# Hybrid decoder step on one core: prompt attention heads in pairs on two row halves and two column groups, with the forget bias copied to all partitions by DMA

## The chip, the core and the metric

The kernel runs on one core of one Trainium2 chip. Its time is the device time of one launch in microseconds, the median of several runs.

## What is computed

One inference step of one hybrid layer for a prompt (1 x 256 tokens) and eight samples (8 tokens each, with 256 cached tokens), all float32, width 1024, 16 heads of 64. The part that matters here is the forgetting attention of the prompt:

```
ft = cumsum(logf)                        # per head, over the 256 tokens
for blk in (0, 1):                       # 128 queries each
    sc   = q[blk] @ k[:kend].T * scale   # kend = 128, then 256
    bias = ft[blk, :, None] - ft[None, :kend]
    p    = softmax(where(mask, sc + bias, -inf))
    out  = p @ v[:kend]
```

The query's own term `ft[q]` is the same for a whole row of the softmax, so both kernels add only `-ft[k]` (`Fp`). Around it stand: adaLN gains from a conditioning vector, one input projection (recurrent input, q, k, v, forget logits, two gates), a convolution and RG-LRU scan, the samples' attention over cached pages, an output projection, and a mixture of 32 experts (top 4) in blocks.

## The kernel before, in words

Five engine programs are written out by hand in `hybrid_layer`, one per engine, with semaphores between them. Nothing schedules them: the order is the text's.

`JOBS` is TensorE's list of projections. It ends with v, four rows of gains, q (eight jobs of 16 passes: a float32 matmul is two passes), then `GATES`: eight jobs for `gbT` and eight for `gaT`, one beside each prompt head (`gate_job`, L1355, matmul L1361). Weights come in chunks of 128 x 8 x 512 floats (2 MB), three buffers in turn. SP issues chunk c when chunk c - 3 has been used (`chunk`, L335). Chunks 18 and 19 hold q, 20 to 23 the gates, 24 and 25 the output projection.

The heads of the prompt, TensorE L1373 to L1410: `scores(h)` writes bank h % 3 with four matmuls, q and k of the head (64 rows, the upper or lower half of the array by h % 2; L1379) and, for the bias, a one-hot column of `ident` against `Fp` (16 rows, L1380), for 128 and for 256 keys. VectorE's `head_max` (L880) adds `mask` and takes two maxima, ScalarE's `exps` (L580) exponentiates, `head_norm` (L890) divides, TensorE's `weights` (L1383) turns three squares of 128, ScalarE copies them out (L592), and `values` (L1391) multiplies them with v in `tok`: 64 columns, the pair's two heads in the two halves of bank 7 one iteration apart. `head_out` (L897) gates a pair and frees the bank. Three heads are in flight in `Ssb`.

```
for h in range(H):          # TensorE, L1404
    gate_job(h)
    if h + 2 < H:
        scores(h + 2)
    if h >= 1:
        values(h - 1)
    weights(h)
```

After it come the cached forget logits (L1419, L1421), their cumulative sum `Fs` on VectorE (L922 to L930), and the samples: keys turned by `keysT`, scores by `sscores` (L1449). `work` first holds the convolution's input and the scan's `A` and `U`, later the samples' `KT`; `rg_free` tells that the scan is over. `F_made` tells that `Fp` (1) and `Fs` (2) are made.

SP's order around the stage: chunks 7 to 21, sixteen small copies of cached forget rows (L357), chunks 22 to 25, then the pages of keys and values.

Of the kernel before, what the change touches and what calls it, by code (L numbers as in the profile page):

```python
# [31 lines left out]
def hybrid_layer(nc, x_prompt, x_sample, cache_k, cache_v, cache_logf, state_conv, state_h, page_table,  # L32
# [35 lines left out]
    with ctx:  # L68
# [32 lines left out]
        Ssb = fr[:, 0:1152].rearrange("p (s n) -> p s n", s=3)  # L101
# [24 lines left out]
        U = Uf.rearrange("p (t c) -> p t c", t=NT)  # L126
        vrows = work[:, 5900:6540].rearrange("p (g n) -> p g n", g=5)
# [81 lines left out]
        Fs = hf[:, 0:2 * (PAST + DS)].rearrange("p (s c) -> p s c", s=2)  # L209
# [8 lines left out]
        nm = few(66, 6).rearrange("p (s n) -> p s n", s=3)  # L218
        rsum = few(72, 6).rearrange("p (s n) -> p s n", s=3)
# [22 lines left out]
        def vec(name, n=NT):  # L242
# [7 lines left out]
            scores_ps scores_read negmax_made exp_done probs_made PT_ps PT_ev py_ps py_read  # L250
# [64 lines left out]
        def _(eng):  # L315
# [23 lines left out]

            for c in range(7):  # L340
                chunk(c)
# [11 lines left out]
            for c in range(7, 22):  # L353
                chunk(c)
# [4 lines left out]
            for c in range(22, len(CHUNKS)):  # L359
                chunk(c)  # L360
            eng.wait_ge(s["rg_free"], 1)

# [15 lines left out]

            keys_in(0)
            keys_in(1)  # L380
            for b in range(DB):
                values_in(b)
                if b + 2 < DB:
                    keys_in(b + 2)
# [29 lines left out]
        def _(eng):  # L414
# [46 lines left out]
            eng.wait_ge(s["rg_free"], 1)  # L461
            for i in range(2):
                eng.tensor_copy(KT[:, i, :, PAST:PAST + NS], kT[:, :, SP_:T]).then_inc(s["tailk_made"], 1)
# [51 lines left out]
        def _(eng):  # L515
# [50 lines left out]
            for j in range(GATES):  # L566
                job(j)
                if j == LAST["f"]:
                    eng.wait_ge(s["absw_made"], 2)
                    A_(Ssb[0:H, 0, 0:T], Ssb[0:H, 0, 0:T], ACT.Exp, scale=-1.0).then_inc(s["expw_made"], 1)  # L570
# [9 lines left out]
            def exps(h):  # L580
                eng.wait_ge(s["negmax_made"], h + 1)
                P = Ssb[:, h % 3, :]
                link(A_(P[:, 0:128], P[:, 0:128], ACT.Exp, bias=nm[:, h % 3, 0:1], accum_out=rsum[:, h % 3, 0:1]))
                A_(P[:, 128:384], P[:, 128:384], ACT.Exp, bias=nm[:, h % 3, 1:2],
                   accum_out=rsum[:, h % 3, 1:2]).then_inc(s["exp_done"], 1)

            exps(0)
            exps(1)
# [115 lines left out]
        def _(eng):  # L704
# [123 lines left out]
            w_, t_, x_ = Ssb[0:H, 1, 0:T], Ssb[0:H, 0, 0:T], Ssb[0:H, 2, 0:T]  # L828
# [13 lines left out]
            for g in range(4):  # L842
                q = 32 * g
                V_.tensor_copy(hsel[q:q + H, :].rearrange("k (h c) -> k h c", c=DS),
                               ident[q:q + H, q:q + H].unsqueeze(2).to_broadcast([H, H, DS])).then_inc(s["hsel_made"], 1)

# [22 lines left out]
            eng.wait_ge(s["consts_made"], 5)  # L869
            link(V_.tensor_tensor_scan(Fp, onesf[0:H, 0:SP_], lfz[:, 0:SP_], 0.0, ALU.mult, ALU.add))  # L870
            TS(Fp, Fp, -1.0, None, ALU.mult).then_inc(s["F_made"], 1)
            ada_rows(8)
            ada_rows(9)
# [3 lines left out]
            ada_rows(10)  # L877
            ada_rows(11)

            def head_max(h):  # L880
                eng.wait_ge(s["scores_ps"], h + 1)
                if h >= 3:
                    eng.wait_ge(s["PT_ps"], h - 2)
                P = Ssb[:, h % 3, :]
                TTo(P, B[h % 3][:, 0:384], mask, ALU.add).then_inc(s["scores_read"], 1)
                eng.wait_ge(s["scores_read"], h + 1)
                link(V_.tensor_reduce(nm[:, h % 3, 0:1], P[:, 0:128], AX.X, ALU.max, negate=True))
                V_.tensor_reduce(nm[:, h % 3, 1:2], P[:, 128:384], AX.X, ALU.max, negate=True).then_inc(s["negmax_made"], 1)

            def head_norm(h):  # L890
                eng.wait_ge(s["exp_done"], h + 1)
                P, r_ = Ssb[:, h % 3, :], rsum[:, h % 3, :]
# [15 lines left out]
            head_max(0)  # L908
            head_max(1)
            for h in range(H):  # L910
                head_norm(h)
                if h + 2 < H:
                    head_max(h + 2)
                if h % 2 and h >= 3:
                    head_out(h // 2 - 1)
                if h > NT:
                    gated(h - NT - 1)
            gated(NT - 1)
            eng.sem_inc(s["rg_done"], 1)

            eng.wait_ge(s["tr_ps"], G_CF + 1)
            link.later(V_.tensor_copy(Fs[:, :, 0:PAST], B[2][:, :].rearrange("p (s c) -> p s c", s=2)))  # L922
# [7 lines left out]
            TS(Fs, Fs, -1.0, None, ALU.mult).then_inc(s["F_made"], 1)  # L930
            head_out(H // 2 - 1)
# [290 lines left out]
        def _(eng):  # L1222
# [128 lines left out]
            eng.wait_ge(s["st_made"], 1)  # L1351
            for g in range(G_ST, G_CF):
                transposes(g)

            def gate_job(h):  # L1355
                j = GATES + h
                eng.wait_ge(s["job_ev"], j - 1)
# [10 lines left out]
            eng.wait_ge(s["F_made"], 1)  # L1368
            eng.wait_ge(s["tr_ev"], G_CF)
            eng.wait_ge(s["adaF_made"], 8)  # L1370
            eng.wait_ge(s["job_ev"], GATES)

            def scores(h):  # L1373
                p, o = h // 2, 64 * (h % 2)
                if h >= 3:
                    eng.wait_ge(s["scores_read"], h - 2)
# [27 lines left out]
            for h in range(H):  # L1404
# [3 lines left out]
                if h >= 1:  # L1408
                    values(h - 1)
# [359 lines left out]
```

## Time and profile before

| | us |
|---|---|
| median of 3 runs | 1550.29 (1547.12 to 1553.09) |
| the profiled execution | 1547.08 |
| its span | 1545.4 |
| TensorE busy, matmuls | 1430.2 |
| VectorE, ScalarE, GpSimd busy | 341.8, 231.4, 25.3 |

The span is the time from the first to the last instruction of the profiled execution. A busy TensorE is no TensorE at its peak: the granted clock (PEclk) can be half, and passes of few columns can wait for their weights. The stages are, by the chain of waits: projections and scan to 263, the heads of the prompt 264 to 416, the samples and the router to 583, the experts to 1530.

### The profile page before, as it was taken

What the parts mean: (1) busy time and instruction counts of PE and PEld (TensorE: products, weight loads), DVE (VectorE), ACT (ScalarE), POOL (GpSimd) and SP (SyncE); (2) the same over time, 40 slices, a digit from 0 to 9 for tenths busy, and PEclk for the clock granted to TensorE, in tenths of its full rate; (3) what the DMA queues carried; (4) which work ended last, traced back from release to release, by engine and by line L of the source; (5) the groups of instructions that cost most, each with busy time, mean ns of one, the idle gap of its engine ahead of it and who ended that gap; (6) DMA issues with size and microseconds to landing.
All of it is one profiled execution on the core that took longest, in us unless ns stands there. A gap on an engine that the chain in (4) does not pass through costs nothing.

```text
span 1545.4 us, 15974 instructions
## 1 busy us (share of the span) xinstructions
PE 1430.2 (93%) x6379; PEld 655.4 (42%) x6379; DVE 341.8 (22%) x693; ACT 231.4 (15%) x461; POOL 25.3 (2%) x55
## 2 busy tenths in 40 slices
PE   6899899999898899999999999999999999999996
PEld 2555356555544643443443433433433433433332
DVE  3441411222323421210210210210120111121114
ACT  2112301211134321110111110111110101100102
POOL 1100001000000010000000000000000000000000
PEclk9899799888998879999999999999999999999999
DMA  8736354111323576999999999999999999999992
GB/s 297 229 142 244 117 218 150 55 55 59 112 82 110 178 322 261 420 429 427 426 428 428 426 427 421 427 428 427 426 428 426 425 428 413 424 430 428 427 426 91
DMA packets 68252, 483.67 MB, mean 313 GB/s; under 512 B 10237, under 2 KB 10981, under 8 KB 43604
## 3 DMA queue, kind: packets, MB, share of 16 engines
q1 hardware_dynamic: 66500, 477.69, 75.4%
q0 software_dynamic: 1680, 4.91, 1.0%
q8 instruction: 58, 0.95, 0.2%
q14 instruction: 14, 0.11, 0.0%
HBM read 478.48 MB, written 4.10 MB: 312 GB/s over the span
## 4 chain that ended last, share of the span: by engine, by line
PE 75%; DMA 17%; DVE 3%; issue 2%; ACT 2%; SPq 1%; DVEq 0%; ACTq 0%; PEldq 0%
PE bank L1683 33%; DMA ring<-in_w_gate_up_dram 17%; PE bank L1334 9%; PE bank L1361 5%; PE bank L1648 4%; PE bank L1226 4%; PE bank L1649 3%; PE bank L1671 2%; PE bank L1517 2%; PE bank L1317 2%; PE bank L1379 1%; PE bank L1380 1%; PE bank L1474 1%; PE bank L1397 1%; PE bank L1449 1%
## 5 line engine op out<-in xcount | busy, mean ns | idle before, releaser
L1683 PE MATMUL bank<-ring,work 128*64 128x512 f32 x2048 | 454.1, 596 | 19.6 <-issue 10.1
L1683 PEld LDWEIGHTS bank<-ring,work 128*64 128x64 f32 x2048 | 160.8, 137 | 291.2 <-issue 291.1
L1683 PE MATMUL bank<-ring,hT 128*64 128x512 f32 x1024 | 235.4, 606 | 16.4 <-DMA ring<-in_w_gate_up_dram 16.4
L1203 DVE TENSOR_TENSOR gbT<-gbT,bank 128x512 f32<-128x512 f32 x85 | 58.4, 687 | 449.0 <-PE bank L1671 388.4
L1334 PE MATMUL bank<-hT,ring 128*128 128x320 f32 x512 | 143.5, 440 | 5.7 <-DVEq L780 4.9
L1683 PEld LDWEIGHTS bank<-ring,hT 128*64 128x64 f32 x1024 | 77.4, 139 | 162.6 <-issue 162.6
L1334 PEld LDWEIGHTS bank<-hT,ring 128*128 128x128 f32 x512 | 97.8, 193 | 53.3 <-issue 6.8
L1172 DVE TENSOR_SCALAR work<-bank 128x512 f32<-128x512 f32 x32 | 22.0, 686 | 328.4 <-PE bank L1683 328.4
L1361 PE MATMUL bank<-hT,ring 128*128 128x320 f32 x256 | 82.2, 480 | 0.0
L1648 PE MATMUL bank<-qT,tok 128*128 128x256 f32 x256 | 72.4, 405 | 0.0
L1671 PE MATMUL bank<-work 128*128 128x512 f32 x136 | 67.4, 618 | 1.2 <-ACT work L694 1.2
L682 ACT ACTIVATE work<-bank 128x320 f32<-128x320 f32 x16 | 7.0, 437 | 407.7 <-PE bank L1226 407.7
L1361 PEld LDWEIGHTS bank<-hT,ring 128*128 128x128 f32 x256 | 54.0, 217 | 22.8 <-issue 7.9
L1648 PEld LDWEIGHTS bank<-qT,tok 128*128 128x128 f32 x256 | 43.4, 189 | 32.2 <-issue 28.9
L694 ACT ACTIVATE work<-bank 128x512 f32<-128x512 f32 x32 | 17.4, 594 | 217.6 <-PE bank L1683 217.6
L1226 PE MATMUL bank<-ident,ring 128*128 128x128 f32 (+2 forms) x187 | 35.6, 338 | 11.5 <-ACT work L601 7.4
L1226 PE MATMUL bank<-ident,work 128*128 128x128 f32 (+3 forms) x205 | 36.0, 299 | 10.6 <-DMA work<-in_state_conv_dram 10.6
L685 ACT ACTIVATE work<-work 128x512 f32<-128x512 f32 x32 | 20.2, 630 | 170.6 <-DVE work L1172 170.6
L1649 PE MATMUL bank<-qT,tok 64*128 64x256 f32 x128 | 44.5, 428 | 0.0
L1317 PE MATMUL bank<-ring 128*32 128x512 f32 x192 | 29.6, 709 | 13.5 <-ACT gbT L544 7.0
L1671 PEld LDWEIGHTS bank<-work 128*128 128x128 f32 x136 | 22.9, 189 | 45.1 <-issue 41.7
L1226 PEld LDWEIGHTS bank<-ident,work 128*128 128x128 f32 (+3 forms) x205 | 25.1, 184 | 32.9 <-issue 32.6
(334 smaller groups left out, 954.4 us busy)
## 6 DMA issues: line engine op xcount, KB each, us to landing
ring<-in_w_gate_up_dram SPq DMA_DIRECT2D x128, 2048.0 KB, 15.0
ring<-in_w_down_dram SPq DMA_DIRECT2D x64, 2048.0 KB, 17.1
ring<-in_w_ada_dram SPq DMA_DIRECT2D x12, 2048.0 KB, 8.0
ring<-in_w_in_dram SPq DMA_DIRECT2D x12, 2048.0 KB, 9.9
ring<-in_cache_k_dram SPq DMA_DIRECT2D x16, 512.0 KB, 5.6
ring<-in_cache_v_dram SPq DMA_DIRECT2D x16, 512.0 KB, 4.5
ring<-in_w_out_dram SPq DMA_DIRECT2D x2, 2048.0 KB, 7.7
out_dram<-tok POOLq DMA_DIRECT2D x2, 1024.0 KB, 5.2
```

What stands on the lines that cost most here:

```text
L685: A_(sig[:, 512 * j:512 * j + 512], glu[:, 512 * j:512 * j + 512], ACT.Sigmoid, scale=ALPHA)\
L1172: TS(glu[:, half[j]], B[j][:, :], LIMIT, None, ALU.min).then_inc(s["glu_made"], 1)
L1203: TTo(piece(gbf, n), piece(gbf, n), B[6 + n % 2][:, :], ALU.add).then_inc(s["scatter_read"], 1)
L1226: return nc.tensor.transpose(out, in_, ident[0:rows, 0:rows])
L1317: last = mm(ps[32 * g:32 * g + 32, :], silu_c[:, k, :], w[0][:, k, :], start=(k < 4), stop=(k >= 4))
L1334: last = mm(ps[:, 0:T], w[0][:, k, 128 * (t % 4):128 * (t % 4) + 128], hT[:, k, :], start=(k == 0), stop=(k == NT - 1))
L1361: last = mm(B[4 + h % 2][:, 0:T], w[0][:, k, 128 * (h % 4):128 * (h % 4) + 128], hT[:, k, :], start=(k == 0), stop=(k == NT - 1))
L1517: last = mm(B[5 + t][:, :], gaT[:, k, 128 * t:128 * t + 128], w[h][:, k, :], start=(k == 0), stop=(k == NT - 1))
L1648: mm(out, tok[:, k, 128 * m:128 * m + 128], sel[:, k, :], start=(k == 0), stop=False)
L1649: last = mm(out, tok[q:q + 64, 2, 128 * (m % 4):128 * (m % 4) + 128], sel[q:q + 64, 2, :], start=False, stop=True)
L1671: last = mm(bank[:, :], C[:, 128 * k:128 * k + 128], Ysb[:, 512 * (n % 2):512 * (n % 2) + 512], start=True, stop=True)
L1683: last = mm(bank[CAP * x:CAP * x + CAP, :], lhsT[:, CAP * x:CAP * x + CAP], rhs(x), start=start, stop=stop)
```

## The change

- TensorE handles heads in pairs. `scores(p)` issues both heads' matmuls of one size one after the other, on the row halves 0 to 63 and 64 to 127, into banks 2 (p % 2) and 2 (p % 2) + 1, without the bias matmuls. `values(p)` issues both heads' on the two column halves of bank 7. `weights` uses bank 6 alone.
- The bias comes by DMA. SP copies row h of `Fp` to all 128 partitions of `biasF[:, h % 8]`, 128 columns and 256 columns, two transfers a head; VectorE's `masked` adds the causal mask to them, eight heads first, then four and four. `head_max` adds `biasF` in place of `mask`.
- Four heads are in flight. `Ssb` and `biasF` now lie in `work`, behind `rg_free`; `Fs` takes the old place in `ring`.
- `Fp` is made right after the forget logits. The state transposes and the gains' rows 8 to 11 move ahead of the last four q jobs. The cached forget logits and their sum move ahead of the last gate job. POOL's copies of the samples' own keys wait for the heads that use `work`.
- SP's issues are put in another order (below).

```diff
+        biasF = work[:, 0:3072].rearrange("p (s n) -> p s n", s=8)
+        Ssb = work[:, 3072:4608].rearrange("p (s n) -> p s n", s=4)
...
+            def bias_rows(a, z):
+                for h in range(a, z):
+                    row = Fp[h:h + 1, :]
+                    eng.dma_start(biasF[:, h % 8, 0:128], row[:, 0:128].unsqueeze(1).to_broadcast([1, 128, 128])).then_inc(s["bias_in"], 16)
+                    eng.dma_start(biasF[:, h % 8, 128:384], row.unsqueeze(1).to_broadcast([1, 128, 256])).then_inc(s["bias_in"], 16)
...
-            for c in range(7, 22):
+            for c in range(7, 20):
+                chunk(c)
+            eng.wait_ge(s["F_made"], 1)
+            eng.wait_ge(s["rg_free"], 1)
+            bias_rows(0, 8)
+            for c in range(20, 22):
                 chunk(c)
...
+            chunk(22)
+            eng.wait_ge(s["scores_read"], 4)
+            bias_rows(8, 12)
+            chunk(23)
+            eng.wait_ge(s["scores_read"], 8)
+            eng.wait_ge(s["bias_made"], 2)
+            bias_rows(12, 16)
             keys_in(0)
             keys_in(1)
+            values_in(0)
+            for c in range(24, len(CHUNKS)):
+                chunk(c)
...
+            for h in range(4):
+                exps(h)
             for h in range(H):
                 job(GATES + h)
                 eng.wait_ge(s["PT_ps"], h + 1)
-                A_(PTs[:, h % 2, :], B[3 + 3 * (h % 2)][:, 0:384], ACT.Copy).then_inc(s["PT_ev"], 1)
-                if h + 2 < H:
-                    exps(h + 2)
+                A_(PTs[:, h % 2, :], B[6][:, 0:384], ACT.Copy).then_inc(s["PT_ev"], 1)
+                if h % 2 and h + 4 < H:
+                    exps(h + 3)
+                    exps(h + 4)
...
+            def masked(a, z):
+                eng.wait_ge(s["bias_in"], 32 * z)
+                v = biasF[:, a % 8:a % 8 + z - a, :].rearrange("p s (t n) -> p s t n", t=3)
+                for t in (0, 2):
+                    link.later(TTo(v[:, :, t, :], v[:, :, t, :], mask[:, 0:128].unsqueeze(1).to_broadcast([128, z - a, 128]), ALU.add))
+                eng.wait_ge(s["chain_dve"], link.n)
+                eng.sem_inc(s["bias_made"], 1)
...
+            masked(0, 8)
+            for h in range(4):
+                head_max(h)
+            for p in range(NT):
+                head_norm(2 * p)
+                head_norm(2 * p + 1)
+                if p in (2, 4):
+                    masked(4 * p // 2 + 4, 4 * p // 2 + 8)
+                if p + 2 < NT:
+                    head_max(2 * p + 4)
+                    head_max(2 * p + 5)
+                if p >= 1:
+                    head_out(p - 1)
+                if p >= 5:
+                    gated(2 * p - 10)
+                    gated(2 * p - 9)
...
+            def scores(p):
+                eng.wait_ge(s["job_ev"], JOBS.index(("q", p)) + 1)
+                if p >= 2:
+                    eng.wait_ge(s["scores_read"], 2 * p - 2)
                 for c, q, n in ((0, 0, 128), (128, 128, 256)):
-                    mm(B[h % 3][:, c:c + n], qT[o:o + 64, p, q:q + 128], kT[o:o + 64, p, 0:n], start=True, stop=False)
-                    last = mm(B[h % 3][:, c:c + n], row, Fp[:, 0:n], start=False, stop=True)
-                last.then_inc(s["scores_ps"], 1)
+                    for o in range(2):
+                        d = slice(64 * o, 64 * o + 64)
+                        last = mm(B[2 * (p % 2) + o][:, c:c + n], qT[d, p, q:q + 128], kT[d, p, 0:n], start=True, stop=True)
+                        if c:
+                            last.then_inc(s["scores_ps"], 1)
...
+            def values(p):
+                eng.wait_ge(s["PT_ev"], 2 * p + 2)
+                if p >= 1:
+                    eng.wait_ge(s["py_read"], p)
+                for o in range(2):
+                    h = 2 * p + o
+                    mm(B[7][64 * o:64 * o + 64, 0:256], tok[:, 0, HD * h:HD * h + HD], PTs[:, o, 0:256], start=True, stop=False)
+                for o in range(2):
+                    h = 2 * p + o
+                    last = mm(B[7][64 * o:64 * o + 64, 128:256], tok[:, 1, HD * h:HD * h + HD], PTs[:, o, 256:384], start=False, stop=True)
+                last.then_inc(s["py_ps"], 1)
...
             scores(0)
             scores(1)
-            for h in range(H):
-                gate_job(h)
-                if h + 2 < H:
-                    scores(h + 2)
-                if h >= 1:
-                    values(h - 1)
-                weights(h)
+            for p in range(NT):
+                gate_job(2 * p)
+                if p >= 1:
+                    values(p - 1)
+                weights(2 * p)
+                if p == NT - 1:
+                    cached_logf()
+                gate_job(2 * p + 1)
+                weights(2 * p + 1)
+                if p + 2 < NT:
+                    scores(p + 2)
```

SP's issues before, up to chunks 18 to 21 (`x4`), which follow each other:

```order
L338 DMA ring<-in_w_in_dram 128x8x512
L338 DMA ring<-in_w_ada_dram 128x8x512 x2
L338 DMA ring<-in_w_in_dram 128x8x512
L338 DMA ring<-in_w_ada_dram 128x8x512 x2
L338 DMA ring<-in_w_in_dram 128x8x512 x4
```

and in the change, up to chunks 18 and 19 (`x2`) and the first two heads' bias rows (`work<-ring`, L345 and L346 of the changed text), a pair of rows that stands eight times before chunks 20 and 21 follow:

```order
L340 DMA ring<-in_w_in_dram 128x8x512
L340 DMA ring<-in_w_ada_dram 128x8x512 x2
L340 DMA ring<-in_w_in_dram 128x8x512 x2
L345 DMA work<-ring 128x1x128
L346 DMA work<-ring 128x1x256
L345 DMA work<-ring 128x1x128
L346 DMA work<-ring 128x1x256
```

Chunks 20 and 21 have moved behind sixteen transfers of bias rows, and chunk 23 and the keys behind eight each.

TensorE, one head in the middle of the stage before (L1361 is the gate's projection, L1226 the three transposes):

```order
L1361 MATMUL bank<-hT,ring 128x320 x8
L1379 MATMUL bank<-kT,qT 128x128
L1380 MATMUL bank<-ring,ident 128x128
L1379 MATMUL bank<-kT,qT 128x256
L1380 MATMUL bank<-ring,ident 128x256
L1397 MATMUL bank<-ring,tok 64x256
L1398 MATMUL bank<-ring,tok 64x128
L1226 MATMUL bank<-ident,ring 128x128 x3
```

and a pair of heads in the change, where L1397, L1432, L1435, L1262 and L1414 are its gate, values, transposes and scores:

```order
L1397 MATMUL bank<-hT,ring 128x320 x8
L1432 MATMUL bank<-ring,tok 64x256 x2
L1435 MATMUL bank<-ring,tok 64x128 x2
L1262 MATMUL bank<-ident,work 128x128 x3
L1397 MATMUL bank<-hT,ring 128x320 x8
L1262 MATMUL bank<-ident,work 128x128 x3
L1414 MATMUL bank<-kT,qT 128x128 x2
L1414 MATMUL bank<-kT,qT 128x256 x2
```

The scores of a pair stand together behind its last transposes, and the values behind the next pair's first gate. On VectorE, at the third pair, the mask addition for heads 8 to 11 (L905) stands behind two divisions and ahead of the maxima of heads 8 and 9 and of the gating of pair 1 (L929):

```order
L924 TENSOR_SCALAR work<-work,tiny 128x256
L905 TENSOR_TENSOR work<-work,ring 128x4x128 x2
L914 TENSOR_TENSOR work<-bank,work 128x384
L916 TENSOR_REDUCE tiny<-work 128x1
L917 TENSOR_REDUCE tiny<-work 128x1
L914 TENSOR_TENSOR work<-bank,work 128x384
L916 TENSOR_REDUCE tiny<-work 128x1
L917 TENSOR_REDUCE tiny<-work 128x1
L929 SCALAR_TENSOR_TENSOR gbT<-gbT,bank 128x256
```

Before, the gating of a pair stands behind one head's maxima and no addition of rows that come by DMA.

## Rows read from the trace of the kernel before

**Rows 1.** The page's second part: granted clock and traffic in 40 slices.

```profile
PEclk9899799888998879999999999999999999999999
...
GB/s 297 229 142 244 117 218 150 55 55 59 112 82 110 178 322 261 420 429 427 426 428 428 426 427 421 427 428 427 426 428 426 425 428 413 424 430 428 427 426 91
```

**Rows 2.** Windows: stretch, length, busy us and instructions by engine, PEclk, DMA share, GB/s.

```profile
263.60:416.00 152.40, 140.32 (x492) 87.74 (x492) 38.42 (x119) 30.38 (x95) 2.32 (x5) 0.87 0.20 72
266.00:268.00 2.00, 2.00 (x6) 1.12 (x5) 1.03 (x3) 0.00 (x0) 0.00 (x0) 0.50 0.73 270
```

**Rows 3.** The chain of waits, 260 to 432: start, length, what.

```profile
260.87 1.28 DVE xT L801 x2
...
263.85 0.46 PE bank L1379 x2
...
301.82 0.57 DVE ring L885
...
303.07 0.42 DVE gbT L900
...
303.63 1.09 PE bank L1397 x2
304.71 0.43 PE bank L1398 x2
305.14 0.83 PE bank L1226 x3
305.97 5.97 PE bank L1361 x16
311.95 0.41 PE bank L1379 x2
312.36 0.41 PE bank L1380 x2
312.77 0.63 PE bank L1379 x2
313.40 0.62 PE bank L1380 x2
314.02 0.58 PE bank L1397 x2
314.60 0.22 PE bank L1398 x2
314.82 0.48 PE bank L1226 x3
315.30 4.31 PE bank L1361 x16
...
416.08 0.99 PE bank L1419 x8
...
424.54 0.43 DVE gbT L900
...
431.29 1.21 PE bank L1449 x16
```

**Rows 4.** Groups by form, TensorE, 612 to 616, experts: busy us, mean ns.

```profile
L1683 PE MATMUL bank<-ring,work 128*64 128x512 f32 x16 | 3.8, 598 | 0.0
L1683 PE MATMUL bank<-hT,qT 32*64 32x512 f32 x16 | 1.1, 612 | 0.0
```

**Rows 5.** A window in which chunks 18 to 20 arrive, columns as in rows 2.

```profile
220.00:222.00 2.00, 1.93 (x7) 1.18 (x7) 0.00 (x0) 0.00 (x0) 0.00 (x0) 1.00 1.06 390
```

**Rows 6.** DMA issues: count, size of each, median us to landing.

```profile
ring<-in_cache_logf_dram SPq DMA_DIRECT2D x16, 8.0 KB, 1.7
kT<-in_x_sample_dram POOLq DMA_DIRECT2D x2, 128.0 KB, 5.2
...
xT<-in_g_mix_post_dram POOLq DMA_DIRECT2D x2, 64.0 KB, 4.2
```

**Rows 7.** Timeline of SP's queue from chunk 18 on: start, us, issues.

```profile
212.45 27.13 SPq L338 DMA_DIRECT2D ring<-in_w_in_dram  x4
```

More of the change, by code:

```diff
@@ L867, in _ @@
             V_.tensor_copy(st36[:, :, 1:NR].unsqueeze(3), windows(U, S0 + DS - 1, 1)).then_inc(s["st_made"], 1)
[L869 to L873, printed above, removed]
+            for c in range(8, 12):
+                ada_rows(c)
             eng.wait_ge(s["out_kv"], 32)
@@ L1350, in _ @@
                         transposes(g)
-            eng.wait_ge(s["st_made"], 1)
-            for g in range(G_ST, G_CF):
-                transposes(g)
+                    eng.wait_ge(s["st_made"], 1)
+                    for g in range(G_ST, G_CF):
+                        transposes(g)
             def gate_job(h):
                 j = GATES + h
-                eng.wait_ge(s["job_ev"], j - 1)
+                eng.wait_ge(s["job_ev"], max(j - 1, GATES))
                 if h % 4 == 0:
@@ L1389, in weights @@
                 last.then_inc(s["PT_ps"], 1)
-            def values(h):
-                p, o = h // 2, 64 * (h % 2)
-                eng.wait_ge(s["PT_ev"], h + 1)
-                if h % 2 == 0 and p >= 1:
+            def values(p):
+                eng.wait_ge(s["PT_ev"], 2 * p + 2)
+                if p >= 1:
                     eng.wait_ge(s["py_read"], p)
-                out = B[7][o:o + 64, :]
-                mm(out[:, 0:256], tok[:, 0, HD * h:HD * h + HD], PTs[:, h % 2, 0:256], start=True, stop=False)
-                last = mm(out[:, 128:256], tok[:, 1, HD * h:HD * h + HD], PTs[:, h % 2, 256:384], start=False, stop=True)
-                if h % 2:
-                    last.then_inc(s["py_ps"], 1)
+                for o in range(2):
[5 more added lines that the diff above has]
+                last.then_inc(s["py_ps"], 1)
@@ new lines, in cached_logf @@
+            def cached_logf():
+                eng.wait_ge(s["cachef_in"], 16 * DB * NPG)
+                eng.wait_ge(s["scores_read"], H - 2)
+                for g in range(4):
+                    q = 32 * g
+                    for n in range(2):
+                        for i in range(NPG):
+                            page_ = NPG * (4 * n + g) + i
+                            mm(B[1][q:q + 32, PAST * n + 128 * i:PAST * n + 128 * i + 128], lfcf[:, H * page_:H * page_ + 32], ident[:, :],
+                               start=True, stop=True)
+                    last = mm(B[0][q:q + 32, 0:NS], lftf[0:NS, 2 * H:2 * H + 32], ident[0:NS, 0:NS], start=True, stop=True)
+                last.then_inc(s["tr_ps"], 1)
@@ L1402, in _ @@
             scores(0)
             scores(1)
-            for h in range(H):
-                gate_job(h)
-                if h + 2 < H:
-                    scores(h + 2)
-                if h >= 1:
-                    values(h - 1)
-                weights(h)
-            eng.wait_ge(s["cachef_in"], 16 * DB * NPG)
-            eng.wait_ge(s["scores_read"], H)
-            eng.wait_ge(s["job_ev"], GATES + H)
-            for g in range(4):
-                q = 32 * g
-                for n in range(2):
-                    for i in range(NPG):
-                        page_ = NPG * (4 * n + g) + i
-                        mm(B[2][q:q + 32, PAST * n + 128 * i:PAST * n + 128 * i + 128], lfcf[:, H * page_:H * page_ + 32], ident[:, :],
-                           start=True, stop=True)
-                last = mm(B[0][q:q + 32, 0:NS], lftf[0:NS, 2 * H:2 * H + 32], ident[0:NS, 0:NS], start=True, stop=True)
@@ L1422, in _ @@
-            last.then_inc(s["tr_ps"], 1)
-            values(H - 1)
+            for p in range(NT):
[9 more added lines that the diff above has]
+                    scores(p + 2)
             def keysT(b):
@@ L1483, in sfold @@
                 last.then_inc(s["sy_ps"], 1)
-            eng.wait_ge(s["py_read"], H // 2)
+            eng.wait_ge(s["F_made"], 2)
             keysT(0)
+            values(NT - 1)
+            keysT(1)
             eng.wait_ge(s["tailk_made"], 2)
             eng.wait_ge(s["fold8_made"], 1)
-            keysT(1)
-            eng.wait_ge(s["F_made"], 2)
             eng.wait_ge(s["hsel_made"], 4)
```

85 lines of the change are left out of this document (35 added, 50 removed).

## The prediction, made before the change was timed

> **What bounds the kernel now.** I read the slices of the page, then the windows, then the chain of waits. The page's slices [rows 1] split the run: from the seventeenth slice on the DMA engines move 420 to 430 GB/s without a gap, which is the expert stage streaming its weights; slices eight to eleven move only 55 to 112 GB/s, and there PEclk is 8 or 9. The windows [rows 2] give that stretch, the prompt attention, as 152.4 us with TensorE busy for 140.3, a mean granted clock of 0.87, VectorE busy for 38.4 and ScalarE for 30.4. So TensorE's own chain sets it, and little of it is data. The chain of waits [rows 3] shows what TensorE does. Per head: projections for a gate, 16 passes, 4.31 us; scores 0.42 + 0.63; the bias rows through a 16-row matmul 0.41 + 0.62; values 0.58 + 0.22; three transposes 0.48. That is 7.67 us a head. In every second head it also stops: values of the pair before wait for VectorE (0.57 for the mask, two reductions, then 0.42 at L900), about 1.85 us, and after it the same passes cost 1.09, 0.43, 0.83 and 5.97 instead of 0.58, 0.22, 0.48 and 4.31. A granted clock of 0.50, which is the 1.2 GHz level, stands in 266 to 268, after the stop of 263 [rows 2]. Stop and slow passes together cost near 4.9 us here, and the chain has seven such stops.
>
> The expert stage begins when TensorE frees its buffers, and its stream then runs at a constant rate [rows 1]. I therefore take a microsecond won before it as a microsecond won at the end, and read the sum at one point: the first scores of the sample stage, L1449 at 431.29 [rows 3].
>
> **TensorE's part of the change.** The bias matmuls (L1380, four passes a head) go: 16 x 1.03 = 16.5 us. Two heads' scores now follow each other in 64-row tiles on the two row halves. The trace has no such pair at 64 rows; the bounds are 2.10 us a pair (2 x 1.05, nothing overlaps) and 0.85 (0.64 of streaming, from 0.21 per 128 columns, plus 0.2 for loads). The nearest row is the expert bias at L1683: 16 passes of 512 columns in four row groups and two column halves take 1.1 us, where 16 passes in column halves alone take 3.8 [rows 4]. Row groups that write different banks do run together, and the new pairs use different banks, so I take 0.85. Values of a pair: 1.60 if nothing overlaps, 0.75 if the column halves do, as in the 3.8 us row; I take 0.75.
>
> VectorE's order changes too. It keeps four heads in flight, so the output of a pair (L900) is computed a whole pair ahead of TensorE's need: VectorE has 38.4 us of work in sixteen heads [rows 2], 4.8 a pair, under two gates (8.62). The stops of 1.85 us and their slow passes should go. ScalarE has 3.8 a pair. The probabilities' transposes now share one bank; each is evacuated behind a gate of 4.31 us, cost nothing, or 0.5 us a head if that cover failed.
>
> At the entry, the state transposes, their two copies and two rows of gains (260.87 to 263.85 [rows 3]) move ahead of the last four query jobs: 3 us less, 1 of it paid earlier, and scores start near 261. The early cumulative sum delays VectorE by about 1 us at 110 to 140, where it waits for TensorE; nothing. At the exit, the cached forget rows (4 x 1.22 us from 416.08) move ahead of the last gate, which hides VectorE's 3.6 us of sums (420.98 to 424.54); keys' transposes follow at once. The 0.74 us clearing and the query copies come later on POOL and VectorE, behind 6 us of key transposes.
>
> If nothing else waits: 262.6 (two pairs of scores) + 16 x 4.31 + 16 x 0.48 + 6 x 0.85 + 7 x 0.75 + 4.9 + 1.1 (a first wait for exponentials) = 355.7; the key transposes and a last values take 6.1 more: 361.8 instead of 431.3, **69 us less**.
>
> **The DMA's part.** This is where I expect most of it to be lost. SP now issues two transfers per head, 128 rows of 512 B and 128 of 1 KB, 196.6 KB, and all of them read one partition, the head's own row of `Fp`. No transfer in this trace reads so much from one partition. The bounds: 0.5 us a head, if it ran as the weight stream at 390 GB/s [rows 5]; 9.4 us a head, if each took the landing time that 64 and 128 KB have here, 4.2 and 5.2 us, one after the other [rows 6]. The row nearest to it is the stream: 428 GB/s over 16 engines [rows 1] is 26.8 GB/s for each, which is what one partition is seen to take, and 196.6 KB at 26.8 is **7.35 us a head**. I take that, since sixteen engines that read the same partition can't each have its full rate. The Trainium skill, SBUF — State Buffer, section "Door 1: The DMA port swizzle", says that eight partitions share a port of about 27.2 GB/s; by it a head costs 7.2 us and the time would be some 2 us below my sum, and no run here shows a read of one partition yet.
>
> The queue is in order, so the weights behind the bias rows wait as well (the order of SP's issues stands in the section on the change):
> - Batch one, eight heads. Chunks 18 and 19 are issued from 212.45 on [rows 7] and at 390 GB/s take until 225. Then 8 x 7.35 to 284, and chunk 20 behind them, 2.1 MB, 5.4 us and landing: 290. TensorE stands before its first gate from 262.6: **27 us** lost. VectorE adds the mask (2.7) and takes four maxima (1.3 each) by 293, hidden.
> - Batch two, four heads, starts behind chunks 21 and 22 at about 303 and lands at 333.5. TensorE reaches values of pair 2 at 290 + 10.4 + 2 x 11.2 + 4.3 + 3 (slow clock) = 330. VectorE is held by the mask of heads 8 to 11, and frees it 4.4 us after landing: 338, **8 us** lost.
> - Batch three is issued then, behind chunk 23 (339), and lands at 368.4; values of pair 4 are freed at 372.8, where TensorE wants them at 363.4: **9 us** lost.
> - What is left: 6.9 + 10.3 + 15.2 + 3 of slow clock = 408, and 6.1 to the sample scores: 414.3. Keys and w_out now come behind this queue, at 370 to 388, 20 us before use; nothing.
>
> Saved: 431.3 - 414.3 = 17; I take 3 off for clock and small waits: **14 us**. The profiled execution took 1547.08 us (span 1545.4); the median of the runs is 1550.29, 3.2 more. Its own time becomes 1533, and beside the median I forecast **1536**. Its own range is 1524 to 1550, from 8.2 to 6.6 us a head.
>
> **The rivals.**
> - *The bias rows are hidden.* Batch one and chunk 20 must land by 262.6, so 37.6 us from 225 less 6.4 for the chunk: up to 3.9 us a head, or 50 GB/s, costs nothing. For it: the stream reaches 390 GB/s, and the 64 B packets of the cached forget rows land in 1.7 us [rows 6]. Against it: the single source. It gives 69 less 3: 1550.3 - 66 = **1484**. If the halves overlapped nowhere, TensorE pays 8 x 1.25 + 7 x 0.85 = 16 more: 1500.
> - *The copies are dearer than one partition's rate.* Each microsecond a head is paid sixteen times in the three batches. The 17 us won are gone at 7.35 + 17 / 16 = 8.4 us a head (23 GB/s). At the upper bound of 9.4 the exit is at 447, 16 later than before: **1566**. For it: landing times of 64 KB here are 4.2 us, and small packets shared by many engines; against it: the transfers are in flight together, and latency is paid once.
> - *The change doesn't do what it says*: the halves don't run together. With the queue as the bound it costs only 5 us, as TensorE's work hides under batches two and three: 1541; it lies in the range.
> - *A later stage gives it back*: the expert stream starts with TensorE's release, so I see no such place.
>
> **How the numbers follow.** Copies at one partition's rate 0.55, hidden 0.30, dearer 0.15. A measurement here tells 0.5%, some 8 us. Of the first case 0.7 is faster, 0.25 the same, 0.05 slower; the second is all faster; the third is slower. Faster 0.55 x 0.7 + 0.30 = 0.68, same 0.14, slower 0.18. The range for 8 in 10 reaches from inside the hidden case, 1482, to 1562, inside the dear one.
>
> **What would show it.** Right: bias copies that land 7 us apart from head to head, 59 us for the first sixteen transfers; TensorE idle near 262 to 290 with DMA as releaser at the first gate (L1361 before); VectorE waiting for DMA at the mask additions of heads 8 and 12; score passes of a pair near 0.85 us; PEclk at 1.0 between the stops. Wrong: the first gate starts by 270 (then 1484), or a batch of four takes over 34 us (then slower).

## The result, and the profile after

| | before | after |
|---|---|---|
| median of 9 runs each, us | 1547.12 (1543.2 to 1553.09) | 1536.35 (1527.68 to 1542.24) |
| the profiled execution | 1547.08 | 1541.73 |
| its span | 1545.4 | 1540.0 |
| TensorE busy, matmuls | 1430.2 | 1394.0 |

The ratio is 0.9928 (95% interval 0.9902 to 0.9955): 10.8 us less by the medians. TensorE's busy time fell by 36 us, and most of that was not won. The page's slices of after show where it went: against [rows 1], slices eight to eleven now carry 123 to 131 GB/s where they had 55 to 112, and the granted clock of the eighth is at 6 instead of 8.

```profile
PEclk9899899688998779999999999999999999999998
...
GB/s 295 216 160 224 119 187 62 125 126 123 131 80 164 194 255 313 420 427 428 427 427 427 427 421 429 428 427 427 426 428 421 428 428 400 420 429 427 428 428 92
```

The windows of after, with the columns of [rows 2]:

```profile
232.00:236.00 4.00, 4.00 (x16) 2.83 (x15) 0.00 (x0) 0.44 (x1) 0.00 (x0) 1.00 0.73 26
263.60:416.00 152.40, 101.81 (x467) 68.58 (x468) 45.51 (x133) 32.85 (x98) 0.63 (x2) 0.82 0.66 120
272.00:296.00 24.00, 2.27 (x5) 1.52 (x6) 7.84 (x18) 3.99 (x15) 0.00 (x0) 0.50 0.79 157
350.00:370.00 20.00, 19.70 (x91) 13.19 (x90) 4.19 (x13) 4.89 (x15) 0.00 (x0) 0.98 0.75 26
```

Over the stretch of the prompt attention TensorE is busy for 101.8 us, not 140.3. While bias copies are under way the DMA engines are busy for three quarters of the time and move 26 GB/s; the weight stream moved 390 [rows 5].

SP's queue of after (timeline: start, us, line, what) tells the rest:

```profile
215.03 3.73 SPq L340 DMA_DIRECT2D ring<-in_w_in_dram  x2
218.88 0.86 SPq L345 DMA_DIRECT2D work<-ring  x1
219.78 0.61 SPq L346 DMA_DIRECT2D work<-ring  x1
...
226.84 14.23 SPq L346 DMA_DIRECT2D work<-ring  x1
241.11 11.91 SPq L345 DMA_DIRECT2D work<-ring  x1
...
278.04 8.86 SPq L340 DMA_DIRECT2D ring<-in_w_in_dram  x2
287.95 19.80 SPq L370 DMA_DIRECT2D ring<-in_cache_logf_dram  x16
307.80 0.43 SPq L340 DMA_DIRECT2D ring<-in_w_in_dram  x1
308.28 0.59 SPq L345 DMA_DIRECT2D work<-ring  x1
...
```

The first eight copies are issued in 0.6 to 0.9 us each and the ninth in 2.3; then one issue takes 14.2 us and the next 11.9. Chunk 20 is not even issued before 278.

The chain of waits of after, as in [rows 3]:

```profile
278.04 15.55 DMA ring<-in_w_in_dram
...
293.73 7.40 PE bank L1397 x16
...
316.57 25.98 DMA work<-ring
...
342.57 1.30 DVE work L905 x2
...
361.43 14.13 DMA work<-ring
...
375.58 1.30 DVE work L905 x2
...
380.14 1.12 PE bank L1432 x4
381.25 0.43 PE bank L1435 x4
...
388.86 0.86 PE bank L1414 x8
...
394.22 0.58 PE bank L1432 x4
394.80 0.22 PE bank L1435 x4
395.02 0.48 PE bank L1262 x3
395.50 4.31 PE bank L1397 x16
...
421.40 1.21 PE bank L1489 x16
```

TensorE's three long stops in its timeline; the brackets hold its idle time before the row and what ended it:

```profile
293.73 7.40 PE L1397 MATMUL bank<-hT,ring 128*128 128x320 f32 x16 [28.28 <-DMA ring<-in_w_in_dram]
...
347.12 1.12 PE L1432 MATMUL bank<-ring,tok 128*64 128x256 f32 x4 [12.62 <-DVE gbT L929]
...
380.14 1.12 PE L1432 MATMUL bank<-ring,tok 128*64 128x256 f32 x4 [8.21 <-DVE gbT L929]
```

Three times the chain runs over a transfer: the weights of the first gate (they land at 293.6; TensorE has stood for 28.3 us since its first scores), the rows of heads 8 to 11 and those of heads 12 to 15. Between them it is the chain that was forecast: a pair's scores 0.86 us (L1414), its values 0.80 (L1432, L1435). The sample scores start at 421.40 instead of 431.29, 9.9 us earlier; of these the two profiled executions show 5.4 at the end (spans 1545.4 and 1540.0).

### The profile page after: what moved, and what is told of

Same layout as the page of the kernel before. It is cut to its first block, busy times and chain, and to the rows that moved or that the text cites. A ratio compares the mean times of both kernels' runs of the same rounds, so it can differ in the third digit from the quotient of the medians.

```text
span 1540.0 us, 15894 instructions
## 1 busy us (share of the span) xinstructions
PE 1394.0 (91%) x6315; PEld 636.1 (41%) x6315; DVE 344.2 (22%) x699; ACT 231.6 (15%) x461; POOL 25.4 (2%) x55
## 4 chain that ended last, share of the span: by engine, by line
PE 68%; DMA 20%; SPq 6%; DVE 2%; ACT 2%; issue 2%; DVEq 0%; ACTq 0%; PEldq 0%
PE bank L1723 34%; DMA ring<-in_w_gate_up_dram 15%; PE bank L1370 7%; PE bank L1688 4%; PE bank L1262 4%; SPq L345 3%; PE bank L1711 3%; DMA work<-ring 3%; PE bank L1689 3%; SPq L346 3%; PE bank L1397 2%; PE bank L1557 2%; PE bank L1353 1%; PE bank L1514 1%; DMA ring<-in_w_in_dram 1%
## 5 line engine op out<-in xcount | busy, mean ns | idle before, releaser
L1370 PE MATMUL bank<-hT,ring 128*128 128x320 f32 x512 | 143.4, 440 | 5.6 <-DVEq L802 4.9
L1370 PEld LDWEIGHTS bank<-hT,ring 128*128 128x128 f32 x512 | 98.0, 193 | 53.3 <-issue 7.2
L1397 PE MATMUL bank<-hT,ring 128*128 128x320 f32 x256 | 77.1, 457 | 28.3 <-DMA ring<-in_w_in_dram 28.3
L1397 PEld LDWEIGHTS bank<-hT,ring 128*128 128x128 f32 x256 | 50.5, 203 | 50.3 <-issue 33.8
L1262 PE MATMUL bank<-ident,work 128*128 128x128 f32 (+3 forms) x253 | 45.1, 300 | 11.5 <-DMA work<-in_state_conv_dram 10.3
L1262 PEld LDWEIGHTS bank<-ident,work 128*128 128x128 f32 (+3 forms) x253 | 30.9, 177 | 38.2 <-issue 36.3
L1262 PE MATMUL bank<-ident,ring 128*128 128x128 f32 (+2 forms) x139 | 23.2, 321 | 8.8 <-ACT work L623 7.5
```

The costliest lines, as they stand in the source:

```text
L1262: return nc.tensor.transpose(out, in_, ident[0:rows, 0:rows])
L1370: last = mm(ps[:, 0:T], w[0][:, k, 128 * (t % 4):128 * (t % 4) + 128], hT[:, k, :], start=(k == 0), stop=(k == NT - 1))
L1397: last = mm(B[4 + h % 2][:, 0:T], w[0][:, k, 128 * (h % 4):128 * (h % 4) + 128], hT[:, k, :], start=(k == 0), stop=(k == NT - 1))
```

## The experiments

All are edits of the changed kernel; ratios are against the kernel before. The question of the first four: is it the copies' single source that holds the stage, and what are the pairs worth alone?

**The copies read all partitions.** Same transfers, same packets.

```diff
-                    eng.dma_start(biasF[:, h % 8, 0:128], row[:, 0:128].unsqueeze(1).to_broadcast([1, 128, 128])).then_inc(s["bias_in"], 16)
-                    eng.dma_start(biasF[:, h % 8, 128:384], row.unsqueeze(1).to_broadcast([1, 128, 256])).then_inc(s["bias_in"], 16)
+                    eng.dma_start(biasF[:, h % 8, 0:128], onesf[:, 0:128]).then_inc(s["bias_in"], 16)
+                    eng.dma_start(biasF[:, h % 8, 128:384], onesf[:, 0:256]).then_inc(s["bias_in"], 16)
```

> The same 32 copies, of the same packets (512 B and 1 KB) into the same places at the same points of SP's queue, but each destination partition reads its own partition of a constant tile (all ones) instead of all reading the head's one row: the forget bias is left out. If the one source partition sets the rate (27 GB/s in the trace of the change), the copies run near the 390 GB/s of the weight stream, 0.5 to 1 us a head, the waits of 27, 8 and 9 us go, and the time is 1484 +- 8 us. If small packets or the making of descriptors set it, the windows still show 27 GB/s and the time stays at 1536.

Measured: 1484.01 us (1481.08 to 1485.4), ratio 0.9574 (0.9527 to 0.9621). The window in which it copies, and its chain:

```profile
228.00:232.00 4.00, 4.00 (x15) 2.49 (x14) 0.70 (x1) 0.44 (x1) 0.00 (x0) 1.00 1.13 330
```

```profile
264.06 0.95 PE bank L1413 x8
...
366.48 1.21 PE bank L1488 x16
```

With the source spread, 330 GB/s arrive where the change moves 26, no wait for data is left in the stage, and the sample scores start 54.9 us earlier than in after; the medians differ by 52.3. It is neither the number of transfers nor their small rows.

**One row in HBM as the source.**

```diff
-                    row = Fp[h:h + 1, :]
+                    row = b_ada[0:1, 256 * h:256 * h + 256]
```

> The same packets again, all 128 of a copy read from one and the same row, but the row lies in HBM (a row of b_ada stands in for the head's; the forget bias is left out). If the limit is SBUF's side of one partition, a row in HBM is not bound by it: 1484 +- 8 us. If any single source row is slow because all engines read one address, it stays at 1536, or gets slower.

Measured: 1481.06 us (1477.85 to 1484.24), ratio 0.9566 (0.9519 to 0.9612). The window of this kernel:

```profile
228.00:232.00 4.00, 4.00 (x17) 2.81 (x16) 0.00 (x0) 0.44 (x1) 0.00 (x0) 1.00 0.83 237
```

One row, read 128 times, costs little if it lies in HBM: 237 GB/s.

**No copies.** `bias_rows` does nothing, `masked` is left out, and `head_max` adds `mask`.

> No bias rows are copied and VectorE adds the plain causal mask, as before the change: the forget bias is left out, the pairs, the four heads in flight and all orders stay. This is the change with its DMA free. By the sum of the prediction the sample scores start 69 us before those of the kernel before and the time is 1481 to 1487. If something else than the copies holds the stage (the halves, VectorE's order, ScalarE), it stays above 1500.

Measured: 1483.21 us (1472.56 to 1488.63), ratio 0.956 (0.9495 to 0.9625), within the scatter of the two runs before. Once the copies are fast they cost nothing at all, and so some 1483 is what the pairs and the new order can give.

**The pairs, with the bias as matmuls again.** The result is complete.

```diff
+                    for o in range(2):
+                        h = 2 * p + o
+                        last = mm(B[2 * (p % 2) + o][:, c:c + n], ident[0:H, h:h + 1].to_broadcast([H, 128]), Fp[:, 0:n], start=False, stop=True)
```

> As the kernel without copies, but the bias comes through TensorE as before the change: per pair two times two more matmuls of 16 rows, one-hot column against Fp. Complete result. TensorE pays up to 16 x 1.03 = 16.5 us more than without copies: 1497 to 1503 us if its chain sets the stage. If the 16-row matmuls also cost the overlap of the two halves (the array changes between 64 and 16 rows twice a pair more), another 5 us.

Measured: 1500.31 us (1495.0 to 1504.04), ratio 0.9691 (0.9643 to 0.9739). Its chain, one pair (L1412 are the scores, L1415 the bias, first for 128 keys and then for 256):

```profile
279.91 0.42 PE bank L1412 x4
280.34 0.64 PE bank L1415 x4
280.97 0.63 PE bank L1412 x4
281.61 1.05 PE bank L1415 x4
```

2.74 us a pair against 0.86: the bias matmuls are worth 8 x 1.88 = 15.0 us, by the medians 16 to 17. They don't overlap as the scores do (1.69 us for the two heads, twice 1.03 before). So without any copy the change would have won 3.1%, some 48 us, and taking the bias off TensorE adds the other 17, if the rows come in time. How much of the 48 is the halves' overlap and how much the new order no run separates; by the chains the halves are worth 8 x (2.10 - 0.86) + 8 x (1.60 - 0.80) = 16 us, an estimate.

The next three try ways out, and a fourth the order of the halves.

**Only the 256-column copy.** The mask's addition reads its first 128 columns and makes the narrow part.

```diff
-                    eng.dma_start(biasF[:, h % 8, 0:128], row[:, 0:128].unsqueeze(1).to_broadcast([1, 128, 128])).then_inc(s["bias_in"], 16)
...
-                eng.wait_ge(s["bias_in"], 32 * z)
+                eng.wait_ge(s["bias_in"], 16 * z)
...
-                    link.later(TTo(v[:, :, t, :], v[:, :, t, :], mask[:, 0:128].unsqueeze(1).to_broadcast([128, z - a, 128]), ALU.add))
+                    link.later(TTo(v[:, :, t, :], v[:, :, max(t, 1), :], mask[:, 0:128].unsqueeze(1).to_broadcast([128, z - a, 128]), ALU.add))
```

> Of the two copies of a head only the one of 256 columns stays; VectorE makes the first 128 columns from it while it adds the mask (the first key block is the same in both). Complete result, 131 KB a head instead of 197 KB. At one partition's 26.8 GB/s a head costs 4.9 us. First batch from 229 to 268, chunk 20 behind it to 274.5: 12 us of wait; the second and third batch cost 4 and 3 us more, and the clock some 4: 1484 + 23 = 1507, range 1500 to 1513. If the rate were set by the number of transfers or packets (half as many) rather than by bytes, a head would cost 3.7 us, under the 3.9 that is hidden: 1484 to 1490.

Measured: 1494.36 us (1492.89 to 1496.58), ratio 0.9666 (0.9646 to 0.9686), between the two forecasts: both missed. A window, SP's timeline and TensorE's:

```profile
228.00:236.00 8.00, 8.00 (x32) 5.62 (x31) 0.00 (x0) 0.87 (x2) 0.00 (x0) 1.00 0.80 26
```

```profile
216.06 5.61 SPq L345 DMA_DIRECT2D work<-ring  x8
221.72 20.03 SPq L340 DMA_DIRECT2D ring<-in_w_in_dram  x2
```

```profile
269.19 7.38 PE L1396 MATMUL bank<-hT,ring 128*128 128x320 f32 x16 [6.48 <-DMA ring<-in_w_in_dram]
...
312.00 0.70 PE L1431 MATMUL bank<-ring,tok 128*64 128x256 f32 x4 [2.06 <-DVE gbT L928]
```

The rate is the same 26 GB/s, so it is bytes that count: two thirds of them make batch one end near 260, when TensorE comes. The forecast of 1507 had this batch run from 229 to 268, but here the chunks ahead of it are through by 226 (28 GB/s from then on), and the first mask addition starts at 260.7, 7 us earlier than forecast. What is left is 6.5 us at the first gate and 2.1 at the batch of heads 8 to 11, each with slow passes behind it (7.38 us where 4.31 is usual). A third fewer bytes bring back 42 of the 52 us. The result is complete.

**The rows by way of HBM.** POOL stores `Fp` to a scratch tensor once (its queue waits for `F_made`), SP copies the 256 columns from there. The narrow part is made as in the last one.

```diff
+        Fd = nc.dram_tensor("scratch_fp", (H, SP_), f32, kind="Internal").ap()
...
-                    row = Fp[h:h + 1, :]
+                    row = Fd[h:h + 1, :]
+                    eng.dma_start(biasF[:, h % 8, 128:384], row.to_broadcast([128, 256])).then_inc(s["bias_in"], 16)
...
-            eng.wait_ge(s["F_made"], 1)
+            eng.wait_ge(s["Fd_made"], 16)
...
+            eng.wait_ge(s["F_made"], 1)
+            eng.dma_start(Fd, Fp).then_inc(s["Fd_made"], 16)
```

> Fp (16 rows of 1 KB) is first stored to a scratch tensor in HBM by POOL's queue, long before use, and the copies of 256 columns read their row there. Complete result. If the source partition is the only fault of the change, this has the time of the kernel without copies, 1483 +- 6 us. If it keeps some wait (the copies still lie ahead of chunk 20 in the queue: 8 x 131 KB at some 240 GB/s are 4.4 us), it is hidden, as chunk 20 has 30 us to spare.

Measured: **1482.3 us** (1481.07 to 1482.71), ratio 0.9584 (0.9566 to 0.9602). The result is complete, so this version beats the kernel before by 64 us and the change by 54. Its window, in which the last copies and the first of chunk 20 arrive together, and its chain:

```profile
228.00:232.00 4.00, 4.00 (x14) 2.32 (x14) 0.70 (x1) 0.44 (x1) 0.00 (x0) 1.00 1.08 353
```

```profile
366.94 1.22 PE bank L1491 x16
```

**Chunk 20 ahead of batch one.** Is it the weights behind the copies, or the copies?

```diff
+            chunk(20)
             bias_rows(0, 8)
-            for c in range(20, 22):
-                chunk(c)
+            chunk(21)
```

> The change with chunk 20 issued ahead of the first eight heads' copies, nothing else. The first gate then runs at 262 to 267 in place of 294 to 301, but the first probabilities still wait for the copies, which now land 5 us later (293), plus mask, four maxima and one division (9 us): the second gate starts near 302 to 305 instead of 301.4. If the weights behind the copies were what costs 27 us, 1515; if the copies themselves reach VectorE as late, 1533 to 1540. I expect 1536.

Measured: 1533.9 us (1532.27 to 1536.54), ratio 0.9919 (0.9897 to 0.9942). TensorE's timeline:

```profile
262.31 4.57 PE L1397 MATMUL bank<-hT,ring 128*128 128x320 f32 x16
297.78 0.90 PE L1262 MATMUL bank<-ident,work 128*128 128x128 f32 x3 [30.89 <-DVE work L924]
298.47 6.16 PE L1397 MATMUL bank<-hT,ring 128*128 128x320 f32 x16
```

The first gate starts at 262, and TensorE then stands for 30.9 us at the first transposes, since the mask waits for the rows. The wait moved by one gate; the medians differ by 2.4 us, and the intervals of the two ratios overlap. So the weights behind the copies are not what costs by themselves: the rows come as late as they do, as forecast.

**Heads one after the other**, on the HBM version: per head both sizes of scores, and both blocks of values, in place of the pair's halves in turn.

```diff
-                for c, q, n in ((0, 0, 128), (128, 128, 256)):
-                    for o in range(2):
+                for o in range(2):
+                    for c, q, n in ((0, 0, 128), (128, 128, 256)):
```

> As the kernel with rows by HBM, but TensorE issues the two heads of a pair one after the other (both sizes of one head, then both of the other, for scores and for values) instead of size by size across the halves. If the alternation is what lets the halves overlap, a pair's scores go from 0.86 to between 1.3 and 2.1 us and its values from 0.80 to between 1.0 and 1.6: 16 x 0.4 to 16 x 1.0 more, 1489 to 1500. If the halves overlap in any order that the hardware finds, less than 3 us.

Measured: 1482.18 us (1479.24 to 1486.68), ratio 0.9576 (0.9553 to 0.96). Its chain still has a pair's values (L1434, L1435) and scores (L1416) at

```profile
295.52 0.59 PE bank L1434 x4
296.11 0.22 PE bank L1435 x4
...
301.44 0.86 PE bank L1416 x8
```

The halves overlap in either order; interleaving the issues brings nothing that can be measured.

The last four ask what the single source shares. Each copy reads `onesf` on a few partitions, every one for 16 or 32 rows. The last two were chosen with the results of the first two known.

```diff
+                    row = onesf[0:8:1]
+                    eng.dma_start(biasF[:, h % 8, 0:128], row[:, 0:128].unsqueeze(1).to_broadcast([8, 16, 128])).then_inc(s["bias_in"], 16)
+                    eng.dma_start(biasF[:, h % 8, 128:384], row[:, 0:256].unsqueeze(1).to_broadcast([8, 16, 256])).then_inc(s["bias_in"], 16)
```

> The source of each copy is eight adjacent partitions (0 to 7 of a tile of ones, sixteen rows of the destination from each) in place of one; the forget bias is left out of the result. Theory A, eight adjacent partitions share one way out: the copies stay at 26 to 28 GB/s in windows 228 to 236 and the time at 1536 (1528 to 1543). Theory B, each partition has its own 26 GB/s: eight of them give up to 8 x 26 = 208 GB/s, a head costs 1 us, below the 3.9 us from which the copies are hidden, and the time is 1484 (1477 to 1490), as with all 128 partitions.

and with `onesf[0:128:16]`:

> The source of each copy is eight partitions 16 apart (0, 16 to 112); the forget bias is left out. Theory A (groups of adjacent partitions share a way out) and theory B (each has its own) both expect up to 208 GB/s and 1484 (1477 to 1490). A third theory, that the engines walk through the rows in step and so meet at one partition whatever the number of sources, expects 26 to 28 GB/s and 1536 here and with the adjacent ones.

Measured: 1482.17 us (1479.8 to 1484.54), ratio 0.955 (0.9495 to 0.9605), and 1483.77 (1483.56 to 1483.98), ratio 0.956 (0.9518 to 0.9601). The same window of either, adjacent first:

```profile
232.00:234.00 2.00, 2.00 (x9) 1.45 (x8) 0.00 (x0) 0.44 (x1) 0.00 (x0) 1.00 0.42 51
```

```profile
232.00:234.00 2.00, 2.00 (x10) 1.37 (x9) 0.00 (x0) 0.34 (x1) 0.00 (x0) 1.00 0.45 91
```

51 and 91 GB/s, neither 26 nor 208: all three theories missed the rate. The prediction's bound, that from 50 GB/s on the copies cost nothing, is nearly met and not quite: with eight adjacent partitions the first gate still waits,

```profile
269.09 5.95 PE L1397 MATMUL bank<-hT,ring 128*128 128x320 f32 x16 [3.69 <-DMA ring<-in_w_in_dram]
```

and its sample scores start at 370.47, against 366.96 with the eight that are 16 apart; the medians of two runs each can't tell 3.5 us. Two rates and one distance suggested groups of four partitions, which the next two tell apart, with `onesf[0:4]` (32 rows each) and `onesf[0:32:4]`.

> The source of each copy is partitions 0 to 3 of the tile of ones; the forget bias is left out. The copies ran at 26 GB/s from one partition, 48 to 51 from partitions 0 to 7 and 87 to 91 from eight partitions 16 apart. Theory C, ways out shared by four adjacent partitions, so that the first had two of them: 26 GB/s again and 1536 (1528 to 1543). Theory D, the rate grows with the number of source partitions, only more slowly than in proportion: between 26 and 50, near 37 GB/s, 5.3 us a head, and 1502 (1495 to 1515). The Trainium skill, SBUF — State Buffer, section "Door 1: The DMA port swizzle", puts partitions 0 to 3 behind one of sixteen ports; by it theory C holds.

> The source of each copy is eight partitions 4 apart (0, 4 to 28); the forget bias is left out. Theory C, ways out shared by four adjacent partitions: eight of them, near 8 x 24 = 192 GB/s (24 from the 48 to 51 of two). Theory D, by the number of source partitions and their distance: between the 50 of eight adjacent and the 90 of eight that are 16 apart, near 60. Either expects 1483 (1477 to 1490), since both are above the 50 GB/s from which the copies are hidden; the window 228 to 236 decides, not the time. By the table of that section of the Trainium skill these eight reach eight ports, and the eight that are 16 apart reach four.

Measured: 1544.41 us (1542.01 to 1551.98), ratio 0.9986 (0.9951 to 1.0022), and 1485.31 (1482.38 to 1488.24), ratio 0.957 (0.9462 to 0.9678). The same window, the four adjacent first:

```profile
232.00:234.00 2.00, 2.00 (x9) 1.41 (x8) 0.00 (x0) 0.00 (x0) 0.00 (x0) 1.00 0.20 23
```

```profile
232.00:234.00 2.00, 2.00 (x9) 1.45 (x8) 0.00 (x0) 0.00 (x0) 0.00 (x0) 1.00 0.56 185
```

Four adjacent partitions give together no more than one (23 against 26), eight that are 4 apart give 185, that is 23 each. So the theory of shared ways out holds on the rate, and the one by the number of partitions (37 and 60) falls. On the time, the 1544.41 lie 1.4 us above its range: the first gate waits for 37.3 us instead of 28.3.

The shape of a copy changes with its sources too, and with it how many engines are at work. The DMA share times 16 gives 11.7 in the change (0.73), 3.2 with four sources (0.20), and 6.7, 7.2 and 9.0 with eight (0.42, 0.45, 0.56). So the cleanest comparison is that of the three with eight sources: the same copies, only the distance differs, and the rates are 51, 91 and 185. The four adjacent ones are not slow for want of engines: one at work moves 23 / 3.2 = 7 GB/s there, against 185 / 9.0 = 21 with eight that are 4 apart and 330 / (1.13 x 16) = 18 with the source spread. By the same figures the 185 may be all that so few engines move, so that it is a lower bound for those eight ways out.

The Trainium skill, SBUF — State Buffer, section "Door 1: The DMA port swizzle", has a table of sixteen ports: partitions 0 to 7 reach two of them, every sixteenth partition four, every fourth of the first 32 eight. The rows agree in order and nearly in size: 26, 51, 91, 185 for 1, 2, 4 and 8 ports, 23 to 26 each, where the page gives 27.2. Groups of four adjacent partitions alone would give the eight that are 16 apart as much as the eight that are 4 apart; the table, which has 0 and 32 on one port, gives them half, as measured (91 against 185). No run reads two such partitions alone.

## Why the prediction was right, and where its terms were off

- **The mechanism.** The likeliest case was copies at one partition's rate, three waits, 14 us less. The rate and the three waits are what happened: TensorE stands for 28.3, 12.6 and 8.2 us, where 27, 8 and 9 were forecast. The cause is shown: the same transfers from a spread source, or from HBM, run without those waits.
- **The rate.** Predicted 7.35 us a head. Batch one: chunks 18 and 19 had arrived near 228 (the traffic is at 387 GB/s until 227, and at 27 from 228 on), and the mask's addition starts at 287.67, so (287.7 - 228) / 8 = 7.5. In the steady window 196.6 KB at 26 GB/s is 7.6 as well. Right, 2 to 3% low. Its source was weaker than its result: 428 GB/s over 16 engines is what one engine moves, and no row of before shows that one partition gives just as much. The run with eight partitions 4 apart and that with four adjacent ones show the limit to be on the side of the source, at 23 to 26.
- **Where the batches begin.** Here the sum was short. SP came to chunk 18 at 215.03, not 212.45 [rows 7]: everything is 3 us later, the first gate at 293.73 instead of 290. Batch two was taken to start at 303 and was issued at 308.28; what held SP was its sixteen small copies of cached forget rows (287.95, 19.8 us), which nobody waited for before. The prediction priced the queue's bytes and left those issues out. It had chunk 22 through by 303; issued at 307.80, just ahead of the batch, its bytes fall inside it. The rows were forecast for 333.5 and came at 342.5, the third batch for 368.4 and came at 375.6, the values of its wait at 380.14 instead of 372.8.
- **The sum.** Sample scores forecast at 414.3 stand at 421.40: 9.9 us saved at that point instead of 17. The profiled execution gained 5.4, the medians 10.8, with the 14 forecast. That 1536 met 1536.35 so closely owes something to luck: the three runs shown then had a median 3.2 us above that of all nine, and the error of the gain is 3 us.
- **A microsecond won before the experts is one at the end.** From the sample scores to the end of the span it takes 1114.1 us before, 1118.6 in the change, 1116.0 with the source spread and 1112.5 by way of HBM. Over the fourteen profiled executions here it lies between 1107.6 and 1118.6, so this step of the sum holds to some 5 us either way, and the 4.5 us by which the profiled pair shows less (5.4 where 9.9 were saved) are within that.
- **TensorE's terms.** Scores of a pair 0.85 forecast, 0.86 measured; values 0.75, 0.80; transposes 0.48 and gates 4.31 as forecast. The case of hidden copies was given 1484, and the spread source gives 1484.01: TensorE's whole sum held to 5 us, with its sample scores at 366.5, not 361.8. The term that failed is the entry, where 3 us were taken off for moving transposes and gains ahead of the last query jobs: the first scores start at 264.06, against 263.85 before. Later small waits make up the rest. The prediction also read seven stops in the chain of before, at 4.9 us each; the chain has six (at 301.82, 321.72, 342.10, 362.33, 381.19 and 400.08), and their distance less two heads of 7.67 is 4.3 us on average. Neither number is in its sum.
- **The rivals.** The copies were not hidden, for the reason given, and the 50 GB/s from which they would be is about right (3.7 us of wait are left at 48 to 51). That the halves don't run together is refuted twice, by after's chain and by the head-by-head run. A dearer copy is seen in the run with four adjacent partitions: 23 GB/s was named as the rate at which the gain is gone, and it gives 0.9986. The 5 us put to that rival of missing overlap (hidden under batches two and three) was not tried.
- **What would show it** did: mask additions waiting for DMA, TensorE idle before the first gate, PEclk at 0.50 in 272 to 296 and at 0.98 in 350 to 370, between the stops. The 59 us forecast for the first sixteen transfers were 60.

## What to carry to other kernels

A copy of one SBUF row to all partitions was bound here by where that row lies, not by the sixteen engines or by the size of its packets: price it at the 23 to 26 GB/s seen here, and if it is wanted, store the row to HBM once and read it from there. Moving the weights ahead of such a transfer brings little (2.4 us here) where the rows themselves are wanted as early. Count in the forecast every issue that the queue makes on the way, the small ones too. When a stage's waits all end on one rate, a third less on that rate can bring back most of the loss, so look for bytes that an engine can make itself.

## What was not expected of the hardware

- An issue on SP's queue can itself take 14.2 us (226.84, usual 0.6), here the tenth copy behind two chunks. The queue's later work then waits at the issue, not only in the engines. The number is no constant: with four adjacent sources already the second copy takes 2.28 us to issue and the fourth 3.80. In the run without the narrow copies all eight were issued in 5.61 us. That the two chunks behind them took 20.03 is no such effect: with the fast copies from HBM they take 17.64, since the second of them waits for its buffer; but the sixteen small copies behind them took 34.69 us instead of 18.91.
- POOL's own stores, two of 256 KB and one of 96 KB, were slowed beside the copies. Before they landed in 5.8 and 4.4 us, in the version by way of HBM in 5.7 and 5.4. The DMA view of after (size, median us to landing):

```profile
out_dram<-tok POOLq DMA_DIRECT2D x2, 256.0 KB, 18.3
out_dram<-xT POOLq DMA_DIRECT2D x1, 96.0 KB, 30.8
```

- The DMA share stood at 0.73 while 26 GB/s moved, and at 0.20 while 23 GB/s moved from four adjacent partitions. The share tells for how much of the time packets were under way, not how much they carried, and GB/s must be read beside it.
